# The last MoE's table of results is read back into two buffers that other expert weights leave, and the final norm scales three of its four tiles in one operation each

## The reference

```python
def run_block(args):                       # one group of rows of one expert
    e, toks, gts = args
    xb = x_pad[toks]
    hid = jax.nn.silu(xb @ w_gate[e]) * (xb @ w_up[e])
    return (hid @ w_down[e]) * gts[:, None].astype(xb.dtype)
...
h = h + hier_moe_2(rmsnorm(h, norm_ffn), ...)      # each token: sum of its two experts' rows
...
def rmsnorm(x, g):
    xf = x.astype(jnp.float32)
    y = xf * lax.rsqrt(jnp.mean(xf * xf, axis=-1, keepdims=True) + RMS_EPS)
    return (y * g.astype(jnp.float32)).astype(x.dtype)
return rmsnorm(h, norm_final)
```

## Time and profile before

| | |
|---|---|
| median of 3 runs | 2462.26 us (2462.26 to 2464.97) |
| profiled execution, its own time | 2464.04 us |
| profiled execution, span from the first to the last instruction | 2462.3 us |
| busy in the span | PE 2158.3 us (88%), DVE 710.3 (29%), ACT 358.8 (15%), POOL 126.7 (5%) |
| moved by DMA | 528.05 MB, 214 GB/s over the span |

### The profile page before, as it was taken

How to read it: one execution, slowest core, us unless ns; L and a number is a source line. 1 busy time by engine, 2 the same in 40 slices (tenths; PEclk the granted TensorE clock), 3 DMA queues, 4 the chain that set the end, 5 groups by cost and what they waited for, 6 DMA issues and landing times.

```text
span 2462.3 us, 27080 instructions
## 1 busy us (share of the span) xinstructions
PE 2158.3 (88%) x11677; PEld 1064.0 (43%) x11677; DVE 710.3 (29%) x1770; ACT 358.8 (15%) x685; POOL 126.7 (5%) x157
## 2 busy tenths in 40 slices
PE   7999999969878877799999999999999697787884
PEld 3455444444333333355666654446444343333331
DVE  2236561251000000403777543021132410000013
ACT  3101220010000000202322442000021100000001
POOL 4000000000000000001110100000000000000000
PEclk9999999979998999899998999999999699999997
DMA  7202102449999999821100102052232499999994
GB/s 258 95 35 78 59 35 102 179 174 403 426 428 427 426 427 427 297 87 26 28 3 2 71 1 86 34 205 103 103 150 102 153 428 427 427 426 427 427 427 162
DMA packets 93003, 528.05 MB, mean 214 GB/s; under 512 B 12896, under 2 KB 27413, under 8 KB 66762
## 3 DMA queue, kind: packets, MB, share of 16 engines
q1 hardware_dynamic: 79008, 492.34, 49.3%
q0 software_dynamic: 10032, 21.22, 2.4%
q10 hardware_dynamic: 3834, 12.64, 1.4%
HBM read 514.02 MB, written 28.31 MB: 220 GB/s over the span
## 4 chain that ended last, share of the span: by engine, by line
PE 67%; DMA 22%; DVE 7%; issue 2%; ACT 1%; ACTq 0%; DVEq 0%; SPq 0%; POOLq 0%
PE ps L198 64%; DMA RING<-in_w 7%; DMA SC<-in_w_e_up 4%; DMA SC<-in_w 4%; DMA RING<-in_w_e_up 3%; DMA XT<-in_w_e_down 3%; DMA SC<-in_w_e_down 1%; DVE X L1747 1%; PE ps L363 1%; PE ps L1362 1%; DMA SC<-ytab 1%; DVE X L1726 0%; PE ps L2707 0%; DMA SC<-xrows,ST 0%; PE ps L2121 0%
## 5 line engine op out<-in xcount | busy, mean ns | idle before, releaser
L198 PE MATMUL ps<-SC 64*64 64x64 f32 (+5 forms) x5904 | 720.2, 330 | 89.8 <-issue 22.5
L198 PE MATMUL ps<-RING,SC 128*64 128x512 f32 (+2 forms) x1872 | 680.1, 617 | 78.2 <-issue 49.0
L198 PE MATMUL ps<-XT,RING 128*128 128x512 f32 x1104 | 493.1, 600 | 6.3 <-DVE SC L2038 3.5
L198 PEld LDWEIGHTS ps<-SC 64*64 64x64 f32 (+3 forms) x5904 | 347.0, 146 | 335.1 <-issue 296.3
L198 PEld LDWEIGHTS ps<-RING,SC 128*64 128x64 f32 (+2 forms) x1872 | 238.8, 158 | 379.1 <-issue 379.1
L198 PEld LDWEIGHTS ps<-XT,RING 128*128 128x128 f32 x1104 | 207.7, 192 | 254.6 <-issue 247.3
L1518 DVE TENSOR_TENSOR SC<-SC,ps 128x512 f32<-128x512 f32 x32 | 22.0, 687 | 718.1 <-PE ps L198 718.1
L198 PE MATMUL ps<-XT,SC 128*64 128x512 f32 x352 | 164.6, 623 | 25.1 <-DMA SC<-in_w 14.3
L198 PE MATMUL ps<-RING,XT 128*128 128x512 f32 (+2 forms) x448 | 156.8, 503 | 0.0
L198 PE MATMUL ps<-SC,RING 128*128 128x512 f32 (+2 forms) x448 | 116.2, 426 | 0.1
L198 PEld LDWEIGHTS ps<-RING,XT 128*128 128x128 f32 x448 | 76.6, 196 | 73.6 <-issue 73.2
(11 more groups left out here) (402 smaller groups left out, 1472.2 us busy)
## 6 DMA issues: line engine op xcount, KB each, us to landing
RING<-in_w SPq DMA_DIRECT2D x43, 2048.0 KB, 33.8
SC<-in_w SPq DMA_DIRECT2D x42, 2048.0 KB, 34.3
RING<-in_w_e_gate SPq DMA_DIRECT2D x22, 2048.0 KB, 34.2
SC<-in_w_e_down SPq DMA_DIRECT2D x17, 2048.0 KB, 33.2
RING<-in_w_in SPq DMA_DIRECT2D x16, 2048.0 KB, 8.3
SC<-in_w_e_up SPq DMA_DIRECT2D x16, 2048.0 KB, 34.7
XT<-in_w SPq DMA_DIRECT2D x11, 2048.0 KB, 33.2
RING<-in_w_e_up SPq DMA_DIRECT2D x10, 2048.0 KB, 32.6
```

What stands on the lines that cost most here:

```text
L198: return e.matmul(out, l, r, start=st, stop=sp, skip_group_check=True)
```

## The change

The four buffers of the table, `YB`, are now the two slots in the last two places of the rotation, which `ybs = first[0][7:9]` picks. For `m0` these are slots 5 and 6 as before, with the two swapped in the order of the tiles. For `m1` they are slots 3 and 6: tiles 0 and 1 go to the last slot of RING instead of SC[0:2], and tiles 2 and 3 to SC[0:2] instead of SC[2:4].

In the final norm DVE no longer multiplies tiles 1, 2 and 3 by the gain ahead of the root. It does tile 0 only, which ACT scales as before, and then makes tiles 1, 2 and 3 in one operation each, X * root * gain (`scalar_tensor_tensor`). ACT no longer scales tile 2. The stores go in the order 0, 1, 2, 3.

```diff
-        YB = [SC[:, tt, :] for tt in range(NT)]
+        ybs = first[0][7:9]
+        YB = [slots.views[i][:, n:n + 2 * D] for i in ybs for n in (0, 2 * D)]
...
-            for i in (5, 6):
+            for i in ybs:
                 for f in slots.put(i, ("yb", bi, i), (c, ("X", NT - 1)))[1]:
                     W.wait_ge(*f)
...
         W.wait_ge(*FN.on("nrm", "rs"))
-        for i in (0, 2):
-            W.wait_ge(*FN.on("xg", i))
-            e.activation(fn_Y[:, i, :], fn_Y[:, i, :], AF.Identity, scale=fn_R.y[:, i:i + 1]).then_inc(*FN.up("a", "y", i))
+        W.wait_ge(*FN.on("xg", 0))
+        e.activation(fn_Y[:, 0, :], fn_Y[:, 0, :], AF.Identity, scale=fn_R.y[:, 0:1]).then_inc(*FN.up("a", "y", 0))
...
-        for i in range(NT):
-            W.wait_ge(*M1.on("X", i))
-            e.tensor_tensor(fn_Y[:, i, :], X[:, i, :], fn_g, A.mult).then_inc(*FN.up("v", "xg", i))
+        W.wait_ge(*M1.on("X", 0))
+        e.tensor_tensor(fn_Y[:, 0, :], X[:, 0, :], fn_g, A.mult).then_inc(*FN.up("v", "xg", 0))
         W.wait_ge(*FN.on("sq", NT - 1))
         mean_rsq_v(e, FN, fn_R, "nrm", fn_ss, 1.0 / D, 1e-6)
         W.wait_ge(*FN.on("nrm", "rs"))
-        for i in (1, 3):
-            W.wait_ge(*FN.on("xg", i))
-            e.tensor_scalar(fn_Y[:, i, :], fn_Y[:, i, :], fn_R.y[:, i:i + 1], None, A.mult).then_inc(*FN.up("v", "y", i))
+        for i in range(1, NT):
+            e.scalar_tensor_tensor(fn_Y[:, i, :], X[:, i, :], fn_R.y[:, i:i + 1], fn_g, A.mult, A.mult).then_inc(*FN.up("v", "y", i))
...
-        for i in (1, 0, 3, 2):
+        for i in (0, 1, 2, 3):
```

## The result

| | before | changed |
|---|---|---|
| median | 2462.26 us (2460.32 to 2464.97, 7 runs) | 2453.18 us (2445.98 to 2456.02, 7 runs) |
| span of the profiled execution | 2462.3 us | 2452.3 us |

The ratio is 0.9958, with a 95% interval of 0.9944 to 0.9972: 9.1 us faster in the medians. The forecast was 12.7. The single runs of the changed kernel lie 10 us apart, so one timing doesn't settle the size; the experiments come to that.

What follows compares the result with a forecast made beforehand. Mostly PE and DMA bound the kernel; from 2424.68 its end hangs on the reads and DVE. Terms 9.7 + 3.0 = 12.7 us, so 2462.26 - 12.7 = 2449.6 us, range 2446.5 to 2453.0.

Steps and rivals of the forecast that it cites:

- Part A: Table reads at the end of the second MoE: they go earlier, without the wait for PE, gaining 9.7 us.
- The cover: PE's matmuls at the end of the second MoE stay hidden ahead of the adds, with 1.4 us to spare.
- The load of the gain: SP's load behind the table reads: now waits for pair 15's up weights, at a cost of nothing.
- the term's bounds: Table reads in the second MoE: gain of 9.7 us from below, 10.7 from above.
- The sign that the prediction named: In the changed profile, the second MoE's reads issued about 9.7 us ahead of PE's last down product's end, at 2415.0.
- The pause ahead of the second table tile: DVE's 0.95 us idle in the second MoE, left open: it may stay or go.
- the upper bound: Table reads: the pause goes, since the DMA engines have been busy until the read as in `m0`; 10.7 us.
- Part B: Final norm: root's chain starts 3.38 us earlier, three fused operations follow, the end comes 3.0 us earlier.
- the 2.7 and the 4.8 of the bounds: Last store's issue to landing: 2.7 us with empty queues, 4.8 with a full queue; ends at least 2457.9 and 2460.0.
- the transfers set the end from the first store's issue on: Final stores: limited by the transfer, all four take 6.5 us from the first issue, ending at 2458.9.
- The body: Rival: something in the first 2400 us, instructions unchanged, moves by more than the whole; 3 in 100.
- its widening of the range: The terms' 2447.6 to 2450.7 us widened by about 1 below and 2.3 above, for scatter between three runs before.

Runs made afterwards that it cites:

- the other two: The changed kernel timed again, unchanged: 2450.29 us against 2462.85 for before, and 2450.76 us against 2460.92.
- reads only: Against the kernel before, only the buffers of the table's reads changed, final norm as before: 2454.13 us against 2462.85, ratio 0.9965.
- norm unfused: Against the changed kernel, tiles 1 to 3 scaled and then multiplied by the gain in separate operations behind the root: 2449.54 or 2449.56 us.
- products for two tiles: Against the changed kernel, DVE multiplies tiles 0 and 2 by the gain ahead of the root, ACT scales both: 2449.54 or 2449.56 us.
- without the wait for the landing: Against the changed kernel, no wait for pair 15's down weights ahead of the table's reads, both MoEs: 2446.61 us beside 2450.29, then 2444.61 beside 2450.76.
- the second one of before: The kernel before, unchanged, profiled again: 498.3 us from SP's load of a RING slot near 1960 to the end, first profile 500.9.

## Why the prediction came out as it did

**Part A, the place and the mechanism: right.** The wait for PE at the reads is gone, the landing is what comes last, and nothing took the wait's place. The reads are 9.8 to 10.0 us earlier than in the first profile of before, where the forecast said 9.7. The cover held: no add waits for PE in the changed kernel. In the first MoE it is just used up where the table comes 2.2 us earlier still; in the second no add waits even there. The load of the gain waits for PE's last product with pair 15's up weights (not for DVE, as the prediction has it), and it went right behind the reads, at 2420.27.

**Part A, the size: one profile taken for the kernel.** The step that was too narrow is the term's bounds, "from below, the pattern of `m1` before stays and part A is 9.7". That pattern is two things, PE's down product of 7.1 us and 2.7 us by which PE came late to it; in the profiles of before the second is there only when the lower clock falls on the last up products. The landing comes at the same distance from S in both kinds, so with the other kind the reads gain 7.1 us. The sign that the prediction named, reads 9.7 us ahead of the end of PE's down product, came out at about 7 for the same reason: PE was on time. As both kinds of before occur, the gain to be expected lies between 498.3 - 487.6 = 10.7 and 500.9 - 487.0 = 13.9, and the 11.4 of all runs lies inside. The 12.7 are a little less than the first kind of before gives and too much for the other. The range of 2446.5 to 2453.0 missed the first timing's median of 2453.18 by 0.2 us and holds the other two.

**The pause ahead of the second table tile** is open still. It was 0.95, 1.27, 1.23 and 1.12 us with the old reads, and 0.58, none and none in the changed kernel, none with the reads only and with the norm unfused, 0.61 with products for two tiles, and none without the wait for the landing. So it is shorter or gone where the reads come right behind the weights, which is where the upper bound put its reason, but it isn't gone each time, and why is not shown.

**Part B: right, to 0.1 us.** Forecast 3.0, measured 14.9 - 11.9 = 3.0 in all seven profiles with this norm. The fused operation is 1.23 us where 1.30 was taken from L1747; the difference changes nothing in the sum, since the stores decide. The last store landed 4.1 us after its issue, between the 2.7 and the 4.8 of the bounds. That the transfers set the end from the first store's issue on was an argument in the prediction and is shown by the kernel with two products. Behind the root DVE has 3.68 us for three fused operations, where three scalings (0.75 each in the unfused kernel) would take 2.3; that loss is real and yet doesn't decide, since the products that it replaces were on the path. The Trainium skill (VectorE: DVE Perf Modes, Mode 2×_2P) gives the second tensor as what costs an operation the doubled rate. The trace agrees: 0.75 us for a scaling, 1.23 for the product of two tensors and for the fused operation.

**The body.** No median moved by more than the whole change, to which the prediction gave 3 in 100. But its widening of the range by about 1 and 2.3 us was too narrow a reading of three runs within 2.7 us of one another: the 47 runs of before lie between 2456.75 and 2468.17, and the medians of the changed kernel 2.9 us apart. The start of the second MoE alone scatters by 7.6 us from profile to profile.

## What to carry to other kernels

When a buffer is reused at the end of a rotation, look which slot's last user comes last: here two slots of the same size came free 30 us apart (PE is done with pair 14's down weights before 2394.44 and with pair 15's at 2424.68), and about 10 us of it counted, down to the landing of the last weights. When an early wait is removed, split it into the work that is always there and the lateness of the engine that does it. The second part may belong to this one profile, so a second profile of the kernel before is worth more than a third digit. A transfer need not wait for the one in front of it to land if nothing in the data asks for it: issued behind the weights, the reads left their landing where it was within 0.3 us, and the first table tile came 2.5 us after the landing instead of 4.9.

## What was not expected of the hardware

The expert stage is paced by the transfers so evenly that in the six profiles in which the reads follow the landing of the last weights they go 453.2 to 453.5 us after S, and the landing in the second one of before is at 460.5 - 7.1 = 453.4, whatever PE's clock does in between: reads only has the slow last up products, the others don't. PE's clock, on the other hand, has different courses over the same instructions: 0.50 to 0.59 over pair 15's last up products in three profiles, 0.76 and 0.77 in one, and 1.00 in eight, which have 0.79 or 0.80 over the up products before them.
